# Constants, norm and projection in one block: parameters loaded in the order of use, pieces of the first two column tiles between the norm's transposes

## The reference, cut to what matters

```python
h = rmsnorm(x, norm_mix)                 # x: 1024 + 64 rows of 1024
proj = h @ w_in                          # 1024 x 3916 columns
qa, ka, va, qi, ki, wi, qkv, a_in, b_in, z = jnp.split(proj, offs, axis=-1)
# indexer: score = sum over 4 heads of relu(qi . ki) * wi, for every pair of tokens
_, sel = lax.top_k(score, 256)           # each query keeps 256 keys
# softmax attention over the chosen keys; gated DeltaNet on conv(qkv)
x = x + mix @ w_out
x = x + jnp.square(jax.nn.relu(rmsnorm(x, norm_mlp) @ w_up)) @ w_down
```

## Time and profile before

| | us |
|---|---|
| median of 3 runs | 2382.64 (2381.5 to 2385.27) |
| profiled execution, its own time | 2386.93 |
| span of the profiled execution | 2385.2 |
| busy: TensorE, VectorE, ScalarE, GpSimd | 2031.1, 1284.2, 642.1, 358.5 |
| mean granted clock of TensorE | 0.924 |

### The profile page before, as it was taken

The page is one execution under the profiler, slowest core; times in us unless marked ns, Lnnn a source line. Parts: engine busy times, 40 slices in busy tenths (PEclk is TensorE's granted clock), DMA queues, the critical chain, the costliest instruction groups (busy, mean ns, idle before and its releaser), DMA issues. The chain is left out here.

```text
span 2385.2 us, 31408 instructions
## 1 busy us (share of the span) xinstructions
PE 2031.1 (85%) x11672; PEld 1678.3 (70%) x11672; DVE 1284.2 (54%) x2271; ACT 642.1 (27%) x1308; POOL 358.5 (15%) x414
## 2 busy tenths in 40 slices
PE   2898899881489997769899959889999999999998
PEld 1787799880158886536654417678888888888886
DVE  2155499999455554857533216644444444444446
ACT  3342224663311111135432204421112111112112
POOL 2333424773020000000103320000000000000000
PEclk8899999995679997869999979989999999999999
DMA  4223322110100001070289646221111111111112
GB/s 119 50 72 94 104 77 71 36 27 0 45 1 1 1 1 36 5 247 2 70 263 324 227 143 224 62 88 36 36 36 45 39 59 36 36 36 45 39 51 75
DMA packets 143109, 176.44 MB, mean 74 GB/s; under 512 B 29048, under 2 KB 99705, under 8 KB 142828
## 3 DMA queue, kind: packets, MB, share of 16 engines
q1 hardware_dynamic: 127628, 127.75, 17.3%
q0 software_dynamic: 15328, 46.68, 6.1%
HBM read 155.86 MB, written 18.01 MB: 73 GB/s over the span
## 5 line engine op out<-in xcount | busy, mean ns | idle before, releaser
L2220 PE MATMUL banks<-front_h_hi,front_w_hi 128*128 128x364 f32 (+1 forms) x744 | 254.9, 343 | 29.6 <-POOL front_w_lo L680 29.6
L2220 PE MATMUL banks<-h_hi,ml_up_hi 128*128 128x364 f32 (+1 forms) x768 | 253.0, 329 | 8.7 <-DVE ml_up_lo L2556 8.7
L2220 PE MATMUL banks<-ml_down_hi,ml_hid_hi 128*128 128x512 f32 (+1 forms) x576 | 228.5, 397 | 29.3 <-DVE x L2585 26.9
L2221 PE MATMUL banks<-h_lo,ml_up_hi 128*128 128x364 f32 (+1 forms) x768 | 253.0, 329 | 0.0
L2222 PE MATMUL banks<-h_hi,ml_up_lo 128*128 128x364 f32 (+1 forms) x768 | 252.9, 329 | 0.0
L417 DVE TENSOR_SCALAR_CACHE_REDUCE work<-arena,work 128x1024 bf16<-128x1024 f32 (+6 forms) x224 | 248.1, 1150 | 2.0 <-DVE work L443 0.3
L2221 PE MATMUL banks<-front_h_lo,front_w_hi 128*128 128x364 f32 (+1 forms) x744 | 248.4, 334 | 0.0
L2222 PE MATMUL banks<-front_h_hi,front_w_lo 128*128 128x364 f32 (+1 forms) x744 | 247.9, 333 | 0.0
L2585 DVE TENSOR_TENSOR x<-x,banks 128x512 f32<-128x512 f32 x256 | 171.5, 686 | 123.1 <-PE banks L2222 122.9
L2221 PE MATMUL banks<-ml_down_lo,ml_hid_hi 128*128 128x512 f32 (+1 forms) x576 | 227.2, 394 | 0.0
L2222 PE MATMUL banks<-ml_down_hi,ml_hid_lo 128*128 128x512 f32 (+1 forms) x576 | 227.0, 394 | 0.0
(11 more groups left out here) (385 smaller groups left out, 3542.6 us busy)
## 6 DMA issues: line engine op xcount, KB each, us to landing
upper<-in_cache_v POOLq DMA_DIRECT2D x128, 256.0 KB, 3.9
upper<-in_cache_k SPq DMA_DIRECT2D x128, 256.0 KB, 3.9
arena<-in_w_up SPq DMA_DIRECT2D x32, 512.0 KB, 4.2
arena<-in_w_down SPq DMA_DIRECT2D x32, 512.0 KB, 5.6
work<-in_w_in SPq DMA_DIRECT2D x30, 512.0 KB, 3.9
op_raw<-in_w_out SPq DMA_DIRECT2D x24, 512.0 KB, 3.6
work<-in_x_prompt SPq DMA_DIRECT2D x8, 512.0 KB, 3.9
x<-in_x_prompt SPq DMA_DIRECT2D x1, 4096.0 KB, 15.1
```

Of the source, the lines that this page charges most:

```text
L2220: pe.matmul(out, lh, rh, start=start, stop=False)
L2221: pe.matmul(out, lh, rl, start=False, stop=False)
```

## The change

`stage_constants` and `stage_norm` become empty, and their work moves into the block of `stage_mixer_projection`, so that the block's barriers between the three are gone.

- The constants' table is ordered so that the parts kept as f32 come first; they are loaded straight into their places, the identity alone and first. The other parts are loaded to a stage and cast to bf16 by VectorE after the norm.
- SyncE's order is: identity, x tile 0, `norm_mix`, x tiles 1 and 2, the first weights, the other f32 constants, the bf16 parts, the page table, then x tiles 3 to 8, with weight load 1 behind x tile 3 and weight load 2 behind x tile 6. The eleven other small parameters are issued behind weight load 3. ScalarE waits for them before the first convolution taps.
- The norm's buffers lie elsewhere, and its transposes use PSUM banks 4 to 7.
- Steps 0 to 5 are the pieces of tiles 0 and 1 in turn: (0,0), (1,0), (0,1), (1,1), (0,2), (1,2). TensorE makes steps 0 and 1 after the transposes of x tile 4, steps 2 and 3 after those of x tile 7. ScalarE copies the banks of steps 0 and 1 after x tile 7. The turns of tiles 0 and 1 come at steps 6 to 8.
- `P_AT` is 8, and with it every later step of the scores is one step later.

The diff, cut ("..." marks what is left out):

```diff
+    seq = [(n, j) for j in range(3) for n in range(2)] + [(n, j) for n in range(2, NF) for j in range(3)]
+    kept_at, made_at, count = {}, {}, 0
+    for s, (n, j) in enumerate(seq):
+        count += 1 + (tiles[n][0] == "c" and j != 1)
+        kept_at[n, j], made_at[n, j] = count, s + 1
+    turns = lambda s: [] if s < 6 else [(0, s - 6), (1, s - 6)] if s < 9 else [(seq[s][0] - 1, seq[s][1])]
...
-    P_AT = 7
+    P_AT = 8
...
+    FIRST_PIECES = {4: (0, 1), 7: (2, 3)}
...
-            load(1)
-            for n in range(NF):
+            ident_at, ident_w = CONST_AT["ident"]
+            sp.dma_start(k.c["ident"], a["const"][:, ident_at:ident_at + ident_w]).then_inc(ident_landed, 16)
+            for t in range(3):
+                sp.dma_start(x_in[t], k.load_x(t)).then_inc(loaded[t], 16)
+                if t == 0:
+                    with nc.allow_non_contiguous_dma(reason="small parameters laid over partitions"):
+                        sp.dma_start(k.g_mix, a["norm_mix"].rearrange("a (k p) -> p (a k)", p=P)).then_inc(gain_landed, 16)
+            sp.dma_start(raw[:, :, 0:DI + NI], w[:, :, OFF_KI:OFF_KI + DI + NI]).then_inc(raw_landed, 16)
+            sp.dma_start(raw[:, :, DI + NI:DI + NI + 2 * G], w[:, :, OFF_A:OFF_A + 2 * G]).then_inc(raw_landed, 16)
+            sp.dma_start(k.view(ident_w, F_COLS - ident_w), a["const"][:, ident_w:F_COLS]).then_inc(const_landed, 16)
+            sp.dma_start(bf_stage, a["const"][:, F_COLS:NC_COLS]).then_inc(const_landed, 16)
+            sp.dma_start(k.table[0:1, :], a["page_table"].rearrange("b n -> (b n)").rearrange("(a n) -> a n", a=1)).then_inc(const_landed, 16)
+            for t in range(3, NX):
+                sp.wait_ge(normed, t - 2)
+                sp.dma_start(x_in[t % 3][0:rows_of(t), :], k.load_x(t)).then_inc(loaded[t % 3], 16)
+                if t == 3:
+                    load(1)
+                if t == 6:
+                    load(2)
+            for n in range(1, NF):
                 if n + 2 < NF:
                     load(n + 2)
+                if n == 1:
+                    with nc.allow_non_contiguous_dma(reason="small parameters laid over partitions"):
+                        sp.dma_start(k.g_mlp, a["norm_mlp"].rearrange("a (k p) -> p (a k)", p=P)).then_inc(small_landed, 16)
+                        for j in range(CW):
+                            sp.dma_start(k.conv_w[:, :, j], a["conv_w"][0, j, :].rearrange("(f p) -> p f", p=P)).then_inc(small_landed, 16)
+                    for h in range(G):
+                        sp.dma_start(k.gdn_row[:, h, :], a["norm_gdn_out"].partition_broadcast(P).rearrange("p a n -> p (a n)")).then_inc(small_landed, 16)
+                    sp.dma_start(k.a_row[:, 0:G], a["a_log"].partition_broadcast(P).rearrange("p a n -> p (a n)")).then_inc(small_landed, 16)
+                    sp.dma_start(k.a_row[:, G:2 * G], a["dt_bias"].partition_broadcast(P).rearrange("p a n -> p (a n)")).then_inc(small_landed, 16)
                 if n == 2:
...
-            low(0)
-            low(1)
+            for t in range(NX):
+                r = rows_of(t)
+                for half in range(2):
+                    part, cols = slice(4 * half, 4 * half + 4), slice(t * P, t * P + r)
+                    pool.wait_ge(rounded, 2 * t + half + 1)
+                    pool.tensor_tensor(k.f_lo[:, part, cols], tmp[t % 2][half][:, :, 0:r], k.f_hi[:, part, cols], ALU.subtract).then_inc(rest, 1)
+                if t == 0:
+                    low(0)
+                if t == 3:
+                    low(1)
...
-                s = 3 * n + j
+                s = made_at[n, j] - 1
                 if j == 0:
                     pe.wait_ge(w_lo, n + 1)
+                if n == 0:
+                    pe.wait_ge(rest, 2 * (-(-(at + w) // P)))
                 if s >= NB:
-                    pe.wait_ge(kept, kept_at[(s - NB) // 3, (s - NB) % 3])
+                    pe.wait_ge(kept, kept_at[seq[s - NB]])
...
-            for s in range(3 * NF):
-                n, j = divmod(s, 3)
+            for t in range(NX):
+                r = rows_of(t)
+                pe.wait_ge(normed, t + 1)
+                if t == 0:
+                    pe.wait_ge(ident_landed, 16)
+                if t >= 2:
+                    pe.wait_ge(x_kept, 2 * (t - 1))
+                for f in range(KD):
+                    last = pe.transpose(k.psum[4 + 2 * (t % 2) + f // 4][:, (f % 4) * P:(f % 4) * P + r],
+                                        xn[t % 2][0:r, f * P:(f + 1) * P], k.c["ident"][0:r, 0:r])
+                last.then_inc(x_turned, 1)
+                if t in FIRST_PIECES:
+                    for s in FIRST_PIECES[t]:
+                        product(*seq[s])
+            for s in range(4, 3 * NF):
+                n, j = seq[s]
                 product(n, j)
-                if n:
-                    turn(n - 1, j)
+                for tn, tj in turns(s):
+                    turn(tn, tj)
...
+                if i == 0:
+                    act.wait_ge(small_landed, 16 * n_small)
...
+            def high_x(t):
+                r = rows_of(t)
+                for half in range(2):
+                    act.wait_ge(x_kept, 2 * t + half + 1)
+                    act.copy(k.f_hi[:, 4 * half:4 * half + 4, t * P:t * P + r], tmp[t % 2][half][:, :, 0:r]).then_inc(rounded, 1)
+
+            length(0)
+            for t in range(NX):
+                if t + 1 < NX:
+                    length(t + 1)
+                high_x(t)
+                if t == 0:
+                    high(0)
+                if t == 3:
+                    high(1)
+                if t == 7:
+                    for s in FIRST_PIECES[4]:
+                        keep(*seq[s])
+            for s in range(2, 3 * NF):
+                n, j = seq[s]
                 keep(n, j)
-                if n and j == 0 and n + 1 < NF:
+                if s == 4:
+                    high(2)
+                if s >= 6 and j == 0 and n + 1 < NF:
                     high(n + 1)
-                if n:
-                    keep_turned(n - 1, j)
+                for tn, tj in turns(s):
+                    keep_turned(tn, tj)
                 for i in prompt_items(s):
                     relu(i)
                 y, u = divmod(s - S_AT, S_STEP)
...
+            dve.memset(k.eps, EPS).then_inc(eps_set, 1)
+            norm(0)
+            for t in range(NX):
+                if t + 1 < NX:
+                    norm(t + 1)
+                keep_x(t)
+            dve.wait_ge(const_landed, 16 * 3)
+            dve.tensor_copy(k.b["ident"], k.c["ident"])
+            for name in BF_CONST[1:]:
+                at, w = CONST_AT[name]
+                dve.tensor_copy(k.b[name], bf_stage[:, at - F_COLS:at - F_COLS + w])
...
-                if s == 5:
+                n, j = seq[s]
```

More of the change, by code:

```diff
@@ L108, in constants @@
     at, where = 0, {}
[L109 to L112, removed]
+    names = [n for n in parts if n not in BF_CONST[1:]] + list(BF_CONST[1:])
+    for n in names:
+        where[n] = (at, parts[n].shape[1])
+        at += parts[n].shape[1]
+    return np.ascontiguousarray(np.concatenate([np.asarray(parts[n], np.float32) for n in names], 1)), where
+BF_CONST = ("ident", "level", "first_low", "columns", "attn_causal", "low_big", "low_big_s", "up_big", "up_big_s", "sel_at")
 CONST, CONST_AT = constants()
 NC_COLS = CONST.shape[1]
-BF_CONST = ("ident", "level", "first_low", "columns", "attn_causal", "low_big", "low_big_s", "up_big", "up_big_s", "sel_at")
 F_CONST = tuple(n for n in CONST_AT if n not in BF_CONST[1:])
+F_COLS = sum(CONST_AT[n][1] for n in F_CONST)
 class Map:
@@ L247, in stage_constants @@
 def stage_constants(k):
[L249 to L266, removed]
-            sp.dma_start(k.a_row[:, 0:G], a["a_log"].partition_broadcast(P).rearrange("p a n -> p (a n)")).then_inc(landed, 16)
-            sp.dma_start(k.a_row[:, G:2 * G], a["dt_bias"].partition_broadcast(P).rearrange("p a n -> p (a n)")).then_inc(landed, 16)
-            sp.dma_start(k.table[0:1, :], a["page_table"].rearrange("b n -> (b n)").rearrange("(a n) -> a n", a=1)).then_inc(landed, 16)
[L270 to L276, removed]
-                at, w = CONST_AT[n]
-                dve.tensor_copy(k.c[n], stage[:, at:at + w])
-            for n in BF_CONST:
-                at, w = CONST_AT[n]
-                dve.tensor_copy(k.b[n], stage[:, at:at + w])
@@ L382 @@
+    pass
+def stage_norm(k, tiles, load):
+    k.load_x = load
 class Threshold:
@@ L556, in stage_mixer_projection @@
     assert m.at <= stage_at
+    m = Map(k.xc_at + 2 * TOK + SEQ + 4 * (NPG // 2) * DI)
+    bf_stage = k.view(m.take(NC_COLS - F_COLS), NC_COLS - F_COLS)
+    assert m.at <= stage_at
+    m = Map(k.hT_at)
+    x_in = [k.view(m.take(D), D) for _ in range(3)]
+    xn = [k.view(m.take(D), D) for _ in range(2)]
+    sqr = k.view(m.take(D), D)
+    tmp = [[k.view(m.take(512), 4, P) for _ in range(2)] for _ in range(2)]
+    stat = k.view(m.take(3 * (NT + 1)), 3, NT + 1)
```

(3 more changed lines are left out.)

136 lines of the change are left out of this document (41 added, 95 removed).

## The result

The changed kernel takes 2358.35 us (median of 4 runs, 2357.27 to 2359.73); the kernel before, on the same chip, 2383.95 (4 runs, 2381.5 to 2387.48). The ratio is 0.9892, 95% interval 0.9875 to 0.9909: 25.6 us less, of which the interval leaves 22 to 30. One execution further down (of the kernel with the split and `P_AT` 7) took 3366.05 us at a granted clock of 0.555 and is left out of its line.

What follows compares the result with a forecast made beforehand. VectorE's 309.5 us of threshold passes, hanging on the own products' arrival, were taken as the bound. Own products 24.3 us earlier gave 2386.93 - 24.3 = 2362.6 profiled, 4.3 above the median: 2358.3 us; range 2348 to 2370, chance 0.8.

Steps and rivals of the forecast that it cites:

- VectorE's stretch: VectorE's 309.5 us of threshold passes from the own step to the next stage: change taken as 0, bounds -6 to +6.
- the own step: Projection step 39 (38 before), whose own products VectorE's threshold passes wait for: 274.7 instead of 298.96, -24.3 us.
- Constants: Loads at the kernel's head: first square on ScalarE at 6.8 us instead of 30.28, -23.5; bounds 5.3 and 12.
- Norm with two pieces: Norm loop: two pieces after tile 4 take 10.1 us, holding tile 5's transposes until 38.6; tile 7's come at 44.6.
- Steps 4 to 6: Projection after tile 8: step 4 starts at 59.4, its piece takes 5.9; step 6 made at 73.6 instead of 105.73, -32.1.
- Page batches: GpSimd's three page-load batches delay weight subtractions; third moves to round 10; with the later step 7.4 us given back.
- Rival 1: Page batches give nothing back: lead about 27 us, or about 32 without half-clock starts, 2351 us; chance 0.22.
- Casts: Constants' bf16 casts beside GpSimd's work for tile 8 and weight tile 2: could hold the latter up by 2.23 us.
- Small parameters: Eleven loads behind weight load 3 hold SyncE 14.9 us, until 85, hidden by 1 us: taken as 0, bounds 0 to +10.
- rival 2: Loads at the head are late (x4, x7, weight load 4): 3 to 12 us given back, 2366 us; chance 0.20.
- rival 4: Small parameters block SyncE between weight loads 3 and 4: slower, about 2394 us if held 50 us; chance 0.03.
- Rival 3: VectorE's stage begins no earlier because another wait, pages on SyncE, ends last: 2380 us, within 0.2%; chance 0.05.

Runs made afterwards that it cites:

- the kernel with the split and `P_AT` 7: Changed kernel with both edits, GpSimd's weight subtraction in the middle of its page batches and `P_AT` 7 instead of 8; own at 253.94 us, no median given.
- experiment 3: Against the changed kernel, no pieces are made between the norm's transposes, all steps come after tile 8: 2365.5 us.
- Experiment 1: Against the changed kernel, `P_AT` goes back from 8 to 7 and VectorE's work tied to step 8 goes to step 7: 2353.78 us.
- Experiment 5: Against the changed kernel, GpSimd subtracts for the next weight tile in the middle of its page batches instead of behind them: 2342.09 us.
- experiment 2: Against the changed kernel, only GpSimd's third batch of sample pages is issued in round 9 instead of round 10: 2363.29 us.
- Experiment 7: Against the changed kernel, GpSimd adds the convolution's taps over 4 columns instead of the tile's width: 2333.21 us.
- Experiment 6: Against the changed kernel, VectorE casts the constants after step 5 is made instead of right behind the norm: 2357.53 us, one run.
- experiment 4: Against the changed kernel, the eleven small parameters are issued behind the page table, ahead of x tile 3: 2369.06 us.

## Why the prediction was right

The forecast was 2358.3 us; 2358.35 was measured. Its mechanism holds in the main: VectorE's stretch hangs on the own step, and the lead there is what the head gains less what the batches and the later step take back. One wait was read wrongly without harm to the sum (the third batch, below), and one term was mis-sized (VectorE's stretch). The closeness is partly luck: of the profiled difference it gave 24.3 to the own step and 0 to VectorE's stretch, where 22.7 and 4.8 were measured, and the profiled execution of before lay 3.0 us over its median, this one 1.1 under.

*Constants.* First square 5.40 us, forecast 6.8, bound 5.3: the table is loaded during the wait, as the low bound had it. Gain 24.9, not 23.5.

*Norm with two pieces.* Tile 4's transposes end at 27.8 (28.5), the two pieces and tile 5's transposes come at 37.42 (38.6), tile 7's at 43.00 (44.6). So the insertion holds the pipeline by 9.9 us where 10.1 were forecast, and experiment 3 shows that it pays some 6 us in all. A delay that I had not foreseen hides in this: VectorE's scaling operation waits behind GpSimd's weight subtraction, which now lies inside the norm. VectorE's and GpSimd's timeline of the changed kernel, one engine after the other:

```profile
8.38 0.76 DVE L1006 TENSOR_SCALAR arena<-arena 128x1024 f32<-128x1024 f32 x1
...
30.27 2.29 DVE L1006 TENSOR_SCALAR arena<-arena 128x1024 f32<-128x1024 f32 x1
```

```profile
29.58 2.44 POOL L604 TENSOR_TENSOR front_w_lo<-work,front_w_hi 128x1024 fp32r<-128x1024 f32 x1
```

The same operation takes 0.76 us while GpSimd is idle and 2.29 when it begins inside the subtraction; it ends 0.5 us after it. That one costs nothing, as TensorE is at its two pieces until 37.42. For x tile 2 it is 1.66 us beside the subtraction of weight tile 0, with TensorE idle behind it.

*Steps 4 to 6.* Step 4 starts at 58.10 (59.4), its piece takes 5.7 us (5.9, at the lower clock), step 6 is made at 72.56 (73.6).

*Page batches.* Step 24 at 179.97 (180.5), step 30 at 220.47 (219.3), the third batch behind step 32 from 233.36 (231), step 36 at 259.69 (258.5), own step at 275.93 (274.7). Forecast to be given back: 7.4 us from step 24 to the own step; measured: 31.7 - 23.0 = 8.7. Experiment 1 shows that the later own step is the cause: without it nothing is given back. Experiment 5 shows that the price of the first two batches is the subtraction queued behind them. For the third the forecast has the time right and the wait wrong: TensorE waits 5.46 us for the pages and begins step 36's product at 254.15, right behind their transposes; the subtraction ends at 254.09, so both conditions give the same start to 0.1 us. In the kernel before, TensorE's wait at the second batch was already for the pages (5.68 us). (The terms for batch two add up to 214.1 us, not 213.9.) The forecast's words "the third batch moves from round 9 to round 10" suggest that the round is the cause, and experiment 2 refutes that: in round 9 it costs 3.7 more. Rival 1, batches that give nothing back (own 7 earlier, 2351 us), falls with these rows. It names what experiment 1 has, and there own did come at 265.52.

*VectorE's stretch.* The term that was mis-sized: 0 taken, -4.8 measured, inside its bounds of 6. It isn't the order of the head that sets it. In the five other kernels with P_AT 8, 32 passes and `EARLY` 12 whose taps are whole (experiments 2 to 6) it is 304.80 to 304.95 though own lies anywhere from 257.14 to 287.32; with P_AT 7 it is 309.25 and 309.42. So it hangs on the step numbers. The traces show where. GpSimd's weight subtractions stand at fixed steps, and the own step moved against them. With `P_AT` 7 one begins 5.8 us behind own and one 19.3 us, each 0.2 us ahead of a small operation of VectorE's, which then lasts until the subtraction is done. The timeline of VectorE and GpSimd, experiment 1:

```profile
271.30 2.41 POOL L604 TENSOR_TENSOR front_w_lo<-work,front_w_hi 128x1024 fp32r<-128x1024 f32 x1 [8.30 <-ACT front_w_hi L793]
...
271.51 2.23 DVE L313 TENSOR_SCALAR work<-work 128x3 int32<-128x3 f32 x1
...
285.07 2.20 DVE L313 TENSOR_SCALAR work<-work 128x3 int32<-128x3 f32 x1
```

And of the changed kernel, where the subtractions begin 0.8 and 14.9 us behind own, beside large passes:

```profile
277.43 2.42 POOL L604 TENSOR_TENSOR front_w_lo<-work,front_w_hi 128x1024 fp32r<-128x1024 f32 x1 [9.87 <-ACT front_w_hi L793]
...
279.57 0.31 DVE L313 TENSOR_SCALAR work<-work 128x3 int32<-128x3 f32 x1
```

That is 4.0 us within 22 us of own (2.23 and 2.20 instead of 0.31 and 0.16). The kernel before and all three experiments with `P_AT` 7 have both long operations, at the same distances; none with `P_AT` 8 has either. The forecast's "as before to within a few us" was thus the weak place: a shift of one step, some 5 us, decides it. It was also not quite the same order of passes: with `P_AT` 8 the prompt's and the sample's passes alternate differently in five places. But the first of these comes some 80 us behind own, when 4.4 of the final 4.5 us between experiment 1 and the changed kernel have arisen, so that is not the cause. Experiment 7 thins the convolution's additions and so shows another part of the same delay; no run moves these two subtractions alone.

*Casts.* By the rule of the Trainium skill (SBUF — State Buffer, "Who interferes with whom") they could have cost GpSimd 2.23 us. Experiment 6 has 0.33, so the measurement decides against that price here; the scaling operation above shows a delay of 1.53 us in the other direction, VectorE held by GpSimd.

*Small parameters.* They hold SyncE for 8.4 us, not 14.9: from 68.66 to 77.07, when weight load 4 is issued; forecast 85. SyncE's timeline:

```profile
68.66 0.58 SPq L555 DMA_DIRECT2D arena<-in_norm_mlp  x1
...
77.07 0.43 SPq L529 DMA_DIRECT2D work<-in_w_in  x1
```

But weight load 4 then lands only 8.9 us after its issue, at 86.0, where loads 3 and 5 need 4.1 and 4.0: it does queue behind the small ones, by 4.8 us. ScalarE rounds it at 88.44. So the slack was some 2.5 us, not 1, and by the shorter hold alone it would have been 7. ScalarE waits for no x tile after the first either, so rival 2 falls, and rival 4 with it. Rival 3 falls with the own operation's 22.7 us. The 14.9 us of the earlier trace rows were measured with 3.5 MB of loads in the same queue, and experiment 4 has 11.3; whether these made the difference was not tried by itself.

## What to carry to other kernels

Follow a gain at the head by step number to the engine that ends the stage, and look at what is tied to a step's place in a loop: here a lead of 33 us became 23 because the own step moved by one and because with it the last batch of page loads came so late that TensorE waited 5.46 us for its pages. Read for each such wait what ended it: three waits of 5 to 7 us that look alike had two causes, and the edit that took away two left the third as it was. A batch of issues on a computing engine should have the computation that others wait for in its middle or ahead of it; that was worth 17.6 us here, all in the first two batches. And take a small operation's duration from the same surroundings, as it may be mostly a wait for another engine.

## What the runs showed of the hardware

VectorE's three small integer forms take 56.4 us beside GpSimd's additions and 33.2 when these are cut to 4 columns, with nothing of VectorE's program changed. A single 128x3 operation of 0.16 us takes 2.23 when it begins 0.2 us into a weight subtraction of 2.41, and ends with it, while the large passes beside the same subtractions keep their length (1.27 us for 1024 columns, 277.04 us in the changed kernel). The 128x3 form of L313 has means of 646, 548 and 319 ns in three kernels, the 64x1 form of that line 146 in all. A VectorE operation that is held so is recorded as busy, not as idle: VectorE's 98% in the stretch contain at least 23 us of waiting.

The granted clock of a short stretch need not be the pace of the matmuls in it. In the kernel of experiment 5 the two agree: between 28 and 30 us the clock is 0.62, and its matmuls follow each other every 0.30 us until 29.5 and every 0.166 from there, the step from the level of 1.2 GHz to that of 2.4. In the changed kernel the row above says 1.00 for the same 2 us, yet its matmuls keep the pace of 0.30 us until 31.5. Where a wait of TensorE's is priced by the clock, the distance of the matmuls is the safer row.
